# A transformer block on one core: more tokens gather their expert rows, and part of u is turned during the input projection

## The reference

```python
def _peer_ffn(x, w_q, sub_keys, expert_u, expert_v):
    ...                       # 8 heads choose 16 experts each: 128 of 16384 for every token
    n_sel = PEER_HEADS * PEER_TOPK
    ...
    def chunk(args):
        xc, ic, gc = args
        u = jnp.take(expert_u, ic, axis=0)
        act = jax.nn.gelu(jnp.einsum('cd,cjd->cj', xc, u), approximate=False) * gc
        return jnp.einsum('cj,cjd->cd', act, jnp.take(expert_v, ic, axis=0))
```

## Time and profile before

| | us |
|---|---|
| median of 3 runs (lowest, highest) | 5099.47 (5097.19, 5101.87) |
| the profiled execution | 5100.68 |
| its span | 5099.0 |
| PE busy | 4453.5 (87%) |
| DVE busy | 3163.2 (62%) |
| ACT busy | 1543.0 (30%) |
| POOL busy | 1613.2 (32%) |
| moved by DMA | 909.28 MB, mean 178 GB/s |

### The profile page before, as it was taken

How to read it: one execution, slowest core, us unless ns; L and a number is a source line. 1 busy time by engine, 2 the same in 40 slices (tenths; PEclk the granted TensorE clock), 3 DMA queues, 4 the chain that set the end, 5 groups by cost and what they waited for, 6 DMA issues and landing times. The chain is left out here.

```text
span 5099.0 us, 60536 instructions
## 1 busy us (share of the span) xinstructions
PE 4453.5 (87%) x23108; PEld 3965.4 (78%) x23108; DVE 3163.2 (62%) x4666; ACT 1543.0 (30%) x2477; POOL 1613.2 (32%) x976
## 2 busy tenths in 40 slices
PE   8999999865766498889965599999999999999995
PEld 6888888623435487677754599999999999999995
DVE  2222222266993443469458588888888888888885
ACT  2111111134441232222322233333333333333332
POOL 0000000000452000033520255555555555555552
PEclk9999999976778799999999799999999999999997
DMA  4333333236105443234315998989888898999883
GB/s 157 115 119 123 123 123 123 79 117 149 36 19 168 157 139 143 74 121 137 120 48 159 287 260 263 262 259 261 260 260 261 260 262 262 262 261 261 261 254 128
DMA packets 556411, 909.28 MB, mean 178 GB/s; under 512 B 44680, under 2 KB 398832, under 8 KB 518928
## 3 DMA queue, kind: packets, MB, share of 16 engines
q1 hardware_dynamic: 518672, 635.62, 43.1%
q0 software_dynamic: 36864, 268.45, 16.2%
q10 hardware_dynamic: 640, 2.10, 0.1%
HBM read 809.51 MB, written 96.56 MB: 178 GB/s over the span
## 5 line engine op out<-in xcount | busy, mean ns | idle before, releaser
L102 PE MATMUL h_ps<-h_xs,h_ut 128*128 128x384 f32 x6144 | 1152.8, 335 | 69.0 <-DMA h_xs<-xs_d 62.1
L102 PE MATMUL h_ps<-h_a,h_v 128*128 128x384 f32 x6144 | 1154.1, 335 | 34.5 <-DVE h_a L96 34.5
L102 PEld LDWEIGHTS h_ps<-h_xs,h_ut 128*128 128x128 f32 x6144 | 1078.2, 189 | 71.3 <-DMA h_xs<-xs_d 62.3
L102 PEld LDWEIGHTS h_ps<-h_a,h_v 128*128 128x128 f32 x6144 | 1070.9, 188 | 44.7 <-DVE h_a L96 44.7
L96 POOL TENSOR_TENSOR h_v<-h_v_raw,h_v 128x512 fp32r<-128x512 f32 x512 | 766.9, 1498 | 872.0 <-ACT h_v L95 869.9
L102 PE MATMUL a_ps<-a_xt,a_w 128*128 128x512 f32 x4224 | 960.0, 390 | 7.7 <-DVE a_w L96 7.7
L102 PEld LDWEIGHTS a_ps<-a_xt,a_w 128*128 128x128 f32 x4224 | 794.6, 188 | 172.8 <-issue 7.9
L96 DVE TENSOR_TENSOR h_ut<-h_u_turn,h_ut 128x512 fp32r<-128x512 f32 x512 | 352.3, 688 | 389.9 <-ACT h_ut L95 389.6
L95 ACT ACTIVATE h_v<-h_v_raw 128x512 fp32r<-128x512 f32 x512 | 322.5, 630 | 588.4 <-PE h_ps L102 588.4
L95 ACT ACTIVATE h_ut<-h_u_turn 128x512 fp32r<-128x512 f32 x512 | 323.7, 632 | 569.9 <-PE h_ps L102 469.3
L96 DVE TENSOR_TENSOR a_w<-a_raw,a_w 128x2048 fp32r<-128x2048 f32 x88 | 201.2, 2288 | 452.9 <-issue 230.6
(11 more groups left out here) (306 smaller groups left out, 5341.4 us busy)
## 6 DMA issues: line engine op xcount, KB each, us to landing
h_u_raw<-in_peer_u SPq DMA_DIRECT2D x512, 256.0 KB
h_v_raw<-in_peer_v SPq DMA_DIRECT2D x256, 512.0 KB
a_raw<-in_w_in SPq DMA_DIRECT2D x44, 2048.0 KB
sums_d<-g_grid SPq DMA_DIRECT2D x3, 8192.0 KB
h_gt<-sums_d SPq DMA_DIRECT2D x128, 192.0 KB
proj_t<-a_ob SPq DMA_DIRECT2D x44, 512.0 KB, 2.8
o_raw<-in_w_o SPq DMA_DIRECT2D x16, 1024.0 KB, 5.0
f_raw<-in_peer_w_q SPq DMA_DIRECT2D x8, 2048.0 KB
```

The source lines that it names most:

```text
L102: mm = pe.matmul(out, lhs[a], rhs[b], start=(first and n == 0), stop=(last and n == 2))
```

## The change

Four things, which share memory and loops.

1. FETCH is 192 instead of 128: 64 more tokens gather. Their 128 choices are laid side by side: partitions 0 to 63 hold a choice of the first four heads, 64 to 127 the matching one of the last four, so that 64 more jobs of 128 rows do. There are 192 jobs (JOBS) in 128 steps, three in two steps, every third of the new kind (`job`). Their results land in y_pair, whose two halves finish adds with a matmul. route makes the indices and gates for it and moves the upper 64 rows with two DMAs.
2. DENSE is 320 instead of 384: matmuls of the expert stage, hid, gates and yt have 320 columns; gate_matrix has 80 units; sums_d is smaller.
3. The input projection's loop loads 88 of the 128 blocks of u into the room of xin, turns each on DVE (the 88 loop steps take one each) and stores it to the new DRAM tensor turned_d.
4. In the expert stage the blocks of u come in another order (`block_of`): step s takes block s % 4 * 32 + s // 4. Blocks below 88 are loaded from turned_d with one DMA of 128 rows of 8 KB and split straight from u_raw; the other 40 are turned as before. v pieces follow that order. ut and v have three buffers of each half (WR), rows four (RR).

```diff
+def turn(dve, out, raw, q):
+    return dve.transpose(out.rearrange("p c (g i) -> p g c i", i=32),
+                         raw[:, :, q * P:(q + 1) * P].rearrange("p g (c i) -> p g c i", i=32))
...
+            def load_u(q, r):
+                for z in range(4):
+                    src = uv[q, z] if isinstance(q, int) else uv[bass.ds(q, 1), z].rearrange("b i g j -> (b i) g j")
+                    sp.dma_start(u_raw[r][32 * z:32 * z + 32, :, :], src).then_inc(u_in[r], 16)
+
+            def store_u(q, r):
+                sp.wait_ge(u_turned, q * Q + Q)
...
+                sp.dma_start(dst, u_turn[r]).then_inc(u_stored[r], 16)
+            sp.wait_ge(x_turned, KT)
...
             with sp.Fori(0, NQ // 4 - 1) as i:
...
+                for s in range(4):
+                    if s % 2 == 0:
+                        sp.wait_ge(lo_done, i * 4 + (s + 2))
+                        sp.dma_start(raw[s // 2][:, :, :],
+                                     wv[bass.ds(i * 2 + (2 + s // 2), 1)].rearrange("g p k c -> (g p) k c"))\
+                          .then_inc(raw_in[s // 2], 16)
+                    store_u(i * 4 + s, s % 2)
+                    load_u(i * 4 + (s + 2), s % 2)
+                    if s >= 2:
+                        store(i * 2 + (s - 2), s - 2, ov[bass.ds(i * 2 + (s - 2), 1)].rearrange("g p b t -> (g p) b t"))
...
                     copy(ob[s // 2][:, s % 2, :], ps[:, s, :]).then_inc(out_done[odd], 1)
+                if odd:
+                    eng.wait_ge(u_in[s % 2], i * 128 + 64 * (s // 2 + 1))
+                    eng.wait_ge(u_stored[s % 2], i * 32 + 16 * (s // 2 + 1))
+                    for c in range(Q):
+                        turn(eng, u_turn[s % 2][:, Q * c:Q * c + Q, :], u_raw[s % 2], c).then_inc(u_turned, 1)
...
-DENSE = T - P
+FETCH = P + P // 2
+DENSE = T - FETCH
...
-            for u in range(NQ * (NB - 1)):
+            for u in range(UNITS):
...
-    AR, RR, VR = 7, 3, 3
+    AR, RR, VR, WR = 7, 4, 3, 3
+    JOBS = SEL + PAIR
...
+        def block_of(s):
+            return s % GRP * GROUPS + s // GRP
+
+        def is_raw(s):
+            return block_of(s) >= 88
...
             def load_u(s):
...
+                if s >= 2:
+                    sp.wait_ge(u_lo, Q * (s - 1))
+                b = block_of(s)
+                if is_raw(s):
...
+                else:
+                    sp.dma_start(u_raw[s % 2][:, :].rearrange("p (c e) -> p c e", e=P), turned_d[b])\
+                      .then_inc(u_in[s % 2], 16)
...
             def u_half(s, q):
...
+                n = Q * s + q
+                u_ready(act, s, q)
+                if n >= WR:
+                    act.wait_ge(h_used, n - WR + 1)
...
+                    if s < STEPS:
+                        m, at = divmod(Q * s + q, 8)
+                        if at in (2, 4, 7):
+                            take(3 * m + (2, 4, 7).index(at))
+                        if at in (0, 2, 5):
+                            dot(3 * m + (0, 2, 5).index(at))
...
+                    m, at = divmod(Q * s + q, 8)
+                    if at in (0, 2, 3, 4, 5, 7):
+                        fetch(6 * m + (0, 2, 3, 4, 5, 7).index(at) + RR - 1)
```

More of the change, by code:

```diff
@@ L167, in _ @@
-            for u in range(2):
-                store(NQ // 2 - 2 + u, u, ov[NQ // 2 - 2 + u])
+            def load_u(q, r):
[4 more added lines that the diff above has]
+                sp.wait_ge(u_turned, q * Q + Q)
+                dst = turned_d[q] if isinstance(q, int) else \
+                    turned_d[bass.ds(q, 1)].rearrange("q p c e -> (q p) c e")
+                sp.dma_start(dst, u_turn[r]).then_inc(u_stored[r], 16)
@@ L169, in _ @@
+            for s in range(4):
+                store_u(NQ - 4 + s, s % 2)
+                if s < 2:
+                    load_u(NQ - 2 + s, s % 2)
+                else:
+                    store(NQ // 2 - 4 + s, s - 2, ov[NQ // 2 - 4 + s])
             for u in range(2):
                 sp.wait_ge(stored[u], 16 * (NQ // 4) + 16)
+                sp.wait_ge(u_stored[u], 16 * (NQ // 2) + 16)
         @block.tensor
@@ L1482, in route @@
                    five % ((0,) * 5) + five % ((1,) * 5) + "names cand " + five % ((2,) * 5) +
-                   "shift mask float match0 match1 pick0 pick1 sum0 sum1 index")
-        sm = Steps(hd.sem, hd.end(PH), "first less sum inverse gate gate_first")
+                   "shift mask float match0 match1 pick0 pick1 sum0 sum1 index index_pair")
+        sm = Steps(hd.sem, hd.end(PH), "first less sum inverse gate gate_first gate_pair0 gate_pair1")
+        late_idx, late_gates, late_moved = sb("late_idx", [PAIR, PAIR], U32), sb("late_gates", [PAIR, PAIR]), sem("late_moved")
         exped, xs_stored = sem("exped"), sem("xs_stored")
@@ L1875, in _ @@
             dve.wait_ge(named, 1)
[L1876 to L1877 removed]
+            for u in range(UNITS):
+                n, v = divmod(u + SKIP, NQ)
                 dve.wait_ge(kept, n + 1)
@@ L1913, in experts @@
         rows = [sb(f"rows{r}", [P, D]) for r in range(RR)]
-        x1 = sb("x1", [P, D])
-        dots, acts = sb("dots", [P, SEL]), sb("acts", [P, SEL])
+        x1 = [sb(f"x1_{n}", [P, D]) for n in ("first", "pair")]
+        dots, acts = sb("dots", [P, JOBS]), sb("acts", [P, JOBS])
         ps = ctx.enter_context(nc.psum_tensor("h_ps", [P, 8, T], F32))
@@ L2023, in choice @@
             def choice(j):
+                pair, c = job(j)
                 act.wait_ge(row_used, 2 * j + 1)
@@ L2164, in _ @@
         def _(pool):
-            Setup(pool, const).identity(ident)
+            c = Setup(pool, const)
+            c.identity(ident)
+            c.fill(both[:, :], 0.0)
+            for first in (0, PAIR):
+                c.keep(both[:, :], ALU.not_equal, [[-1, PAIR]], 1, 1.0, base=-first)
+            assert c.n == 5
         @block.sync
@@ L2186, in _ @@
                         pe.wait_ge(summed, j - 6)
+                    first = FETCH - P if n == 1 else 0
+                    t = n * P - FETCH
+                    if first:
+                        pe.matmul(ps[0:first, j % 8, :], both[:, :], y_pair[:, T * g:T * (g + 1)], start=True, stop=True)
                     for i in range(4):
-                        t = pe.transpose(ps[:, j % 8, i * P:(i + 1) * P], yt[:, 4 * g + i, (n - 1) * P:n * P],
-                                         ident[:, :])
-                    t.then_inc(turned, 1)
+                        here, made = yt[:, 4 * g + i, t + first:t + P], ps[first:P, j % 8, i * P:(i + 1) * P]
+                        if first:
+                            tr = pe.matmul(made, here, ident[:, :], start=True, stop=True)
+                        else:
+                            tr = pe.transpose(made, here, ident[:, :])
+                    tr.then_inc(turned, 1)
         @block.scalar
```

243 lines of the change are left out of this document (141 added, 102 removed).

## The result

The changed kernel takes 5152.94 us (median of 4 runs, 5143.72 to 5160.71), the kernel before 5098.33 (5092.96 to 5101.87). The ratio is 1.0107 with a 95% interval of 1.0086 to 1.0129: slower by 1.1%, where 4893 us was forecast. 5153 lies outside the range.

A forecast was written before the change was run, and what follows sets the result against it. DMA was to replace TensorE as the expert stage's bound at 15.5 us a step: 5100.7 - 186 - 7 - 5 - 5 - 29 + 20 + 2 + 2 = 4893 us, range 4740 to 5080.

The forecast's parts named there:

- VectorE's 14.0 us: Expert stage: VectorE busy per step, from 13.8 us before, -1.9 for turns, +2.4 for half a job, about -0.3 for narrower operations.
- rival B: Expert stage: GpSimd becomes the bound, its gathers and halves stretched beside VectorE; step 16.4 us, total 5004 us; chance 0.18.
- Rival C: Expert stage: DMA takes the whole gain back; step 17.7 us, +87, total 5206 us, DMA share 0.95, PE below 86%; chance 0.14.
- The DMA term, 15.5 us: Expert stage: DMA ends last in each of 124 steps, the middle of 14.1 to 16.8 us, against 17.0 before: -186 us.
- rival A: Expert stage: DMA engines keep pace at 424 GB/s with a step of 14.5 us; -310, total 4758 us; chance 0.25.
- The opening, -7: Four opening steps of the expert stage, 12.3 us each before: 7 us less because three of four blocks come turned.
- The gate matrix: Gate matrix stage, VectorE's: 80 units instead of 96 at 1.81 us each, -29 us.
- Matmuls of 148 ns: Expert stage on TensorE: 148.0 ns per 320-column matmul instead of 174.2, so 96 take 14.2 us a step.
- The input projection: Projection stage: added block loads and turned stores make DMA slower than PE, between +13 and +79, taken as +20 us.
- Route: Route stage: ten small VectorE operations and two small moves on SP, +2 us (0 to 5).
- the way to the first matmul: Ahead of the expert stage's opening steps: xs smaller (-2.5 us) and first u block 2.2 us quicker, together -5.
- the tail: End of the expert stage: 192 matmuls each 26.2 ns shorter, -5 us.

The follow-up runs named there:

- GpSimd quiet: Changed kernel with GpSimd making the low half of v for only 8 of every 128 columns, the rest zeroed: 4982.84 us, 0.9766 of before.
- both walls away: Changed kernel with GpSimd's low half of v over 8 of every 128 columns and gathered rows of 4 KB instead of 8 KB: 4734.45 us.

## Why the prediction was wrong

**VectorE's 14.0 us: the step that failed.** The forecast let the DMA engines end last (15.5 us a step) and VectorE hide behind them. It took VectorE's operations at their means in the kernel before, added half a job and found 14.0 us, under TensorE's 14.2. It was 16.1, and with its waits the step was 17.64. The undisturbed sum is lower still, 12.4 us (GpSimd quiet); 3.7 us a step are standstill. The means of before held for the pattern of meetings of that kernel: TensorE set the pace, and the low halves of u ran at 0.69 us on the mean. I had the mechanism in hand as rival B, with the gate multiply's 1.65 us beside GpSimd, and priced it on GpSimd alone. Whichever comes second stands still, and what counts is who has no room: VectorE, with 3.7 us on top of 12.4, had none in a step of 15.5, and GpSimd has 29% to spare even now. The Trainium skill (SBUF — State Buffer, "Who interferes with whom") says that issue order, not the shape of the operation, decides who blocks. The trace agrees: 0.09 us late at 3407.95, and 2.97 - 0.69 = 2.3 us of standstill.

**VectorE's waits and the clock: 1.5 us a step.** These are the rest of the 17.64. Per 1000 us, 57 steps, VectorE waited 47.9 us for ScalarE's high half of u, 23.1 for that of a and 9.9 for TensorE. Much of it follows TensorE's wait once per group:

```profile
3430.23 1.48 PE L102 MATMUL h_ps<-h_a,h_v 128*128 128x320 f32 x9
3437.76 1.17 PE L102 MATMUL h_ps<-h_a,h_v 128*128 128x320 f32 x3 [6.05 <-DVE h_a L96]
3438.73 3.40 PE L102 MATMUL h_ps<-h_xs,h_ut 128*128 128x320 f32 x12
3441.93 2.83 PE L102 MATMUL h_ps<-h_a,h_v 128*128 128x320 f32 x12
3444.60 1.92 PE L102 MATMUL h_ps<-h_xs,h_ut 128*128 128x320 f32 x12
```

After 6.05 us without work the granted clock is at its lower level, 1.2 GHz (0.55 on the mean from 3437.7 to 3444.6), and the first 27 matmuls take 6.84 us, where at the later rate (1.76 us from one twelve to the next) they would take 4.0. That is 2.9 us per group of four steps, 0.7 a step, nearly all by which TensorE's 15.0 busy us a step exceed 14.2. In these microseconds VectorE waited for ScalarE and TensorE 1.57, 1.22 and 2.00 us, 4.8 of the group's 6. The clock fell behind VectorE's delay and did not begin it; no run separates what it added to the step. With both walls away it stood at 1.00.

**Rival C came true in its number and not in its cause.** 17.64 us a step against its 17.7, and its signature almost met (PE at 85%, 306 GB/s, a DMA share of 0.93 instead of 0.95). This was luck. With half of each row gone the time did not fall. So a DMA share of 0.93 at 306 GB/s did not mean here that the DMA engines were the bound; why it stood so high at so few GB/s is not shown.

**The DMA term, 15.5 us.** With VectorE out of the way the step is 15.9 us at a share of 0.99, so the forecast was 0.4 short there; over all 124 steps, with the raw blocks of the last third, it would still have been 0.7 short (span 4980.4 less the 96.6 us behind the steps and the 2874.5 ahead, by 124: 16.2). Of the 266 us between the forecast of the 124 steps and their measure, 0.7 x 124 = 87 us are thus this term's, and the other 179 went away with GpSimd's wide operations. A gather took 0.452 x 1000 / 171 = 2.64 us in the changed kernel (179.24 MB are 171 gathers of 1.05 MB), near the low end of the 2.47 to 3.20:

```profile
q1 hardware_dynamic: 82479, 128.72, 47.5%
q0 software_dynamic: 24613, 179.24, 45.2%
```

The fastest long stretch that I read in any run moved 346 GB/s, with the engines full. The 424 GB/s of the x load lasted 9 us. I kept rival A because of it; a rate of 9 us is no rate for 2000. The Trainium skill's 358 GB/s (DMA: Bandwidth & Descriptors, Specifications) I quoted without its condition: under "Measured" the same page gives it as the share of a core when both cores of a memory domain stream, and 425 GB/s for a load of 16 MB by one core alone. This program runs on one core, so the 424 of the short stretch agrees with the page, and the page's limit is no reason for the 346 of the long one.

**The opening, -7 against +14.4 us.** TensorE ran out after 36 matmuls, 8.88 us, because VectorE sat before its loop for the copies of x1 for the added tokens, behind xs in the queue:

```profile
2823.69 0.69 DVE L96 TENSOR_TENSOR h_ut<-h_u_raw,h_ut 128x512 fp32r<-128x512 f32 x1 [26.08 <-DMA h_x_pair<-x_d]
```

I had not counted these loads; another wait of 7.51 us stands before a raw block that lands late.

**The other terms.** The gate matrix took 146.7 us and not 175.7 (2606.07 to 2781.73): -29.0 against -29. Matmuls of 148 ns held: the run with both walls away has 14.3 us a step at 0.993 busy, 148 ns for each of 96. The input projection cost 3.9 us and not 20: its DMA share is 1.05 at 314 GB/s and TensorE was busy 600.00 of 600 us, so the restarts that I charged did not come. Its last copy ended at 990.6 us, 1.1 earlier than before and not 10 to 40 later; the 3.9 us are the last turn and store behind it. Route came out at -1.8 (+2 forecast), the way to the first matmul at -8.3 (-5), the tail at -0.1 (-5) and the finish at -2.1 (+2). With the 124 steps at +80.1 (-186) and the opening this makes +57.1 us, the difference of the spans.

## What to carry to other kernels

A duration read in one kernel belongs to that kernel's pattern of meetings; when a change makes an engine the bound, price its two-operand SBUF work with GpSimd beside it, or take GpSimd's wide work away from it. If VectorE is the bound and its operations are longer than the same shape elsewhere in the trace, giving it GpSimd's work can be the gain (5153 to 5000 here), and where TensorE is the bound the same move is a loss (5100 to 5135). A DMA share over 0.9 proves nothing by itself (at 0.93 halving the rows gained nothing, at 0.99 it gained 249 us): halve the bytes once while the other wall stands, and once after it is gone.

## What the runs showed of the hardware

GpSimd's low half over 8 of every 128 columns still took 725 ns on the mean:

```profile
L96 POOL TENSOR_TENSOR h_v<-h_v_raw,h_v 128x32 fp32r<-128x32 f32 x252 | 182.8, 725 | 439.1 <-ACT h_v L95 436.8
```

The mean is not what the operation needs. By the view of its tile the shortest took 250 ns, half of them at most 290, the longest 2370. One of 2.25 us started at 3409.02 us, 0.20 us after a take on VectorE (3408.82, 2.34 us), and ended 0.11 us behind it. So the short operation still stands still behind VectorE's long ones, while VectorE's, at 690 and 2303 ns, are hardly stretched by it.

Gathers are stretched too, by what VectorE does beside them. With nothing but gathers on GpSimd (the run with v's low half on VectorE), the view of their line gives for each kind the least, median and longest duration in ns:

```profile
L2257 POOL DMA_INDIRECT h_rows<-in_peer_v,idx_first x62: 932/941/949, 3002.6 to 3985.8; - x62
L2257 POOL DMA_INDIRECT h_rows<-in_peer_u,idx_first x61: 936/939/1312, 3006.4 to 3980.3; - x61
L2257 POOL DMA_INDIRECT h_rows<-in_peer_u,idx_pair x31: 936/936/940, 3018.1 to 3992.1; - x31
L2257 POOL DMA_INDIRECT h_rows<-in_peer_v,idx_pair x30: 1227/2744/2748, 3026.4 to 3966.8; - x30
```

The fourth kind is issued when a take frees its row, and in that slot a dot product follows the take at once, as the timeline shows:

```profile
3026.03 2.29 DVE L2203 CUSTOM_DVE_ANT_0 h_rows<-h_rows,h_x_first 128x2048 f32<-128x2048 f32 x1
3026.38 2.74 POOL L2257 DMA_INDIRECT h_rows<-in_peer_v,idx_pair  x1 [7.29 <-DVE y_first L2212]
```

The dot product has its undisturbed 2.29 us: a gather loses to VectorE and does not hold it up. A low half does the same: the gather of 3029.43 us started 0.19 us after a low half of v on VectorE (3029.24, 0.69 us) and took 1.31 us instead of 0.94. Rival B took from the Trainium skill (SBUF — State Buffer, "SBUF: two separate sides") that descriptors which GpSimd writes wait for VectorE; the page says so of VectorE's operations in a two-port mode, and these rows show it for operations with two operands in SBUF.
